# Attention's steps a turn later, copies behind a projection later, and level products in any free PSUM pair

## What is computed

```python
h = rms_norm_2(x, norm_pre[layer])
proj = h @ w_in[layer]
y_a = gla_branch(...)          # gated linear scan, 4 heads, both directions
for block of 128 queries:      # diff_branch, 4 heads
    s = einsum(q, k)           # two score maps, c = 0 and 1
    p = softmax(s)
    o = (p[0] - lam * p[1]) @ v
y_c = hgrn_branch(...)         # gated linear scan, 4 heads, both directions
y = concatenate([y_a, y_b, y_c]) @ w_out[layer]
x = x + rms_norm_2(y, norm_post[layer])
```

## Time and profile before

| | us |
|---|---|
| runs shown | 4494.43, 4501.37, 4509.14 (median 4501.37) |
| the profiled execution's own time | 4500.21 |
| its span (first to last instruction) | 4498.4 |
| PE / DVE / ACT / POOL busy in the span | 3923.6 / 1992.3 / 1439.2 / 958.7 |
| mean granted PE clock, share of full speed | 0.931 |

### The profile page before, as it was taken

The page is one execution under the profiler, slowest core; times in us unless marked ns, Lnnn a source line. Parts: engine busy times, 40 slices in busy tenths (PEclk is TensorE's granted clock), DMA queues, the critical chain, the costliest instruction groups (busy, mean ns, idle before and its releaser), DMA issues.

```text
span 4498.4 us, 66792 instructions
## 1 busy us (share of the span) xinstructions
PE 3923.6 (87%) x29404; PEld 2409.6 (54%) x29404; DVE 1992.3 (44%) x2165; ACT 1439.2 (32%) x1795; POOL 958.7 (21%) x426
## 2 busy tenths in 40 slices
PE   6988899999989999988997978988787978978777
PEld 3555565666656665455444555555444455555444
DVE  2456455555454642432224354263642264264542
ACT  4222323233232322222113323333444232343442
POOL 2313333232333322031132201111002210111002
PEclk8999999999999999999998988989888989989899
DMA  2111111111111112432212000100012100100002
GB/s 92 53 39 39 48 39 53 39 53 45 43 50 42 57 49 84 159 122 103 104 69 86 30 10 19 33 15 24 19 52 76 34 10 10 43 19 20 24 8 101
DMA packets 61585, 226.93 MB, mean 50 GB/s; under 512 B 6832, under 2 KB 8560, under 8 KB 60784
## 3 DMA queue, kind: packets, MB, share of 16 engines
q1 hardware_dynamic: 50064, 181.77, 11.7%
q10 hardware_dynamic: 11232, 40.90, 2.3%
HBM read 174.93 MB, written 47.71 MB: 49 GB/s over the span
## 4 chain that ended last, share of the span: by engine, by line
PE 71%; DVE 16%; ACT 9%; DMA 2%; issue 1%; POOL 1%; ACTq 0%; DVEq 0%; SPq 0%; POOLq 0%
PE psum L955 69%; DVE arena L2038 6%; ACT arena L1524 5%; DVE arena L2041 4%; DVE arena L2493 2%; DVE arena L2430 2%; PE psum L958 2%; ACT L1524 1%; ACT wh L1524 1%; DMA arena<-in_w_proj_conv 1%; DVE arena L2045 1%; ACT arena L1979 1%; DVE hl L2038 0%; ACT hh L1524 0%; POOL wl L2548 0%
## 5 line engine op out<-in xcount | busy, mean ns | idle before, releaser
L955 PE MATMUL psum<-arena 64*64 64x32 f32 (+11 forms) x19116 | 1589.3, 283 | 390.4 <-ACT arena L1524 186.2
L955 PEld LDWEIGHTS psum<-arena 64*64 64x64 f32 (+5 forms) x19116 | 1109.5, 158 | 878.5 <-issue 448.8
L2548 POOL TENSOR_TENSOR wl<-arena,wh 128x1024 bf16<-128x1024 f32 (+1 forms) x195 | 474.7, 2434 | 2405.4 <-ACT wh L1524 2403.6
L955 PE MATMUL psum<-hh,wh 128*128 128x512 f32 x3120 | 891.4, 432 | 98.6 <-ACT arena L1524 24.7
L1524 ACT ACTIVATE arena<-psum 128x512 f32<-128x512 f32 (+4 forms) x660 | 415.8, 630 | 1393.7 <-PE psum L955 1055.3
L955 PE MATMUL psum<-hh,wl 128*128 128x512 bf16 x3120 | 784.0, 394 | 1.2 <-POOL wl L2548 1.2
L955 PEld LDWEIGHTS psum<-hh,wh 128*128 128x128 f32 x3120 | 607.0, 200 | 301.7 <-issue 58.6
L2038 DVE TENSOR_TENSOR arena<-psum,arena 128x512 f32<-128x512 f32 (+3 forms) x488 | 319.3, 654 | 973.7 <-PE psum L955 628.1
L955 PE MATMUL psum<-hl,wh 128*128 128x512 bf16 x3120 | 736.0, 383 | 5.6 <-POOL hl L2548 5.5
L2041 DVE SCALAR_TENSOR_TENSOR arena<-arena 128x1024 f32<-128x1024 f32 x356 | 573.9, 1612 | 83.1 <-ACT arena L1524 69.9
L2548 POOL TENSOR_TENSOR arena<-arena 128x1024 f32<-128x1024 f32 (+4 forms) x142 | 362.6, 2553 | 955.1 <-ACT arena L1524 467.9
(11 more groups left out here) (38 smaller groups left out, 834.1 us busy)
## 6 DMA issues: line engine op xcount, KB each, us to landing
arena<-in_w_in SPq DMA_DIRECT2D x161, 512.0 KB, 3.5
scr_g<-arena ACTq DMA_DIRECT2D x24, 512.0 KB, 2.6
arena<-scr_g SPq DMA_DIRECT2D x24, 512.0 KB, 4.4
arena<-in_w_out SPq DMA_DIRECT2D x24, 512.0 KB, 3.5
arena<-in_w_mem_kv SPq DMA_DIRECT2D x16, 512.0 KB, 3.5
scr_x<-arena SPq DMA_DIRECT2D x16, 512.0 KB, 3.6
arena<-scr_x SPq DMA_DIRECT2D x16, 512.0 KB, 7.4
arena<-in_x SPq DMA_DIRECT2D x8, 512.0 KB, 10.3
```

The source lines that it names most:

```text
L955: return pe.e.matmul(o, l, r, start=start, stop=stop)
L2548: return pool.seq.tensor_tensor(o, a, b, op)
```

## The change

- `attend`: `dw` is split. `dr` (DVE: reciprocal and the tiny product) comes after `WT`; `e1` (ACT) does the scaling of EX[z] one long step later; `dw` (DVE) keeps the multiply-add alone and stands in the next turn, behind that turn's `qk`. `dmax` and `dexp` follow `qk` after one short step each (a short step advances the fillers once, a long one twice). The score pairs are kept until `dexp`.
- Between `dexp` and `dv` the levels and diagonals may take any of the four pairs (`room`, ANY).
- `copied`: the copy behind eight scan projections a layer and behind all `dvp` and `dqk` projections comes half a yield later, and the pair is kept until then. `dvp`, `dqk` and `dg` projections go in parts of 3 matmuls, each a quarter of a yield.
- `grow`: the two products on KG come first, then the two on QF, then the two of the tree; `xk` and `kt` wait for those on KG, `lev` for those on QF.
- `PACE` and `BESIDE` have other values. Loads are placed up to three ahead. The roots `fin` and `pre0` are made in the other order, `consts2` waits for `pre0`'s sum, and the sum `pre1` of the second layer takes a pair of UPPER instead of LOWER.

```diff
         self.owed += n
         while self.owed >= 1 and self.live:
-            self.owed -= 1
             try:
-                next(self.g)
+                self.owed -= next(self.g) or 1
             except StopIteration:
                 self.live = False
 
...
-        for f, *n in fillers:
-            f.step(n[min(stage or 0, len(n) - 1)])
+    for share in main:
+        for f, n in fillers:
+            f.step(n * (share or 1))
 
 
...
+    LOWER, UPPER, ANY = (0, 4), (4, 8), (0, 8)
...
-    def P(key, src, h, n=S, m=128, back=False, among=LOWER, deep=2):
+    def P(key, src, h, n=S, m=128, back=False, among=LOWER, deep=2, share=None):
 
 
         PROJ[key] = (src, h, n, m, back)
         steps = (n + 511) // 512 * 8 * (1 if h is None else 3)
         deep = deep if h is None else 3 * deep
         for part in range(steps // deep):
-            yield
+            yield share
...
-        for t in tags[::-1]:
+        for t in tags:
             do("stat_sum", t)
             do("stat_end", t)
         ps.leave(("stat", tag))
...
-    def held(step, use):
-
-        ps.take(use, 2, LOWER)
+    def held(step, use, among=LOWER):
+
+        ps.take(use, 2, among)
         ps.keep(use, 2)
         do(*step)
+
+    room = {"levels": LOWER}
+
+    def copied(g, key, *step):
+
+        yield from g
+        ps.keep(("proj", key), 2)
+        yield 0.5
+        do(*step)
+        ps.leave(("proj", key))
 
...
-                do("sv_copy", L, t, i)
+                key = ("sv", L, t, i)
+                yield from copied(P(key, w[ct], f"p{L}", deep=4), key, "sv_copy", L, t, i)
                 yield
...
-                held(("diag", L, t, g, p), ("diag", L, t, g, p))
+                held(("diag", L, t, g, p), ("diag", L, t, g, p), room["levels"])
...
                 for g, p in parts:
-                    held(("lev", L, t, lv, g, p), ("lev", L, t, lv, g, p))
+                    held(("lev", L, t, lv, g, p), ("lev", L, t, lv, g, p), room["levels"])
                     yield
                     if (g, p) == parts[-1]:
                         do("grow", L, t, lv)
...
 
-        yield from P(("dvp", L, h), A["w_in_2"][L][14 + h], f"p{L}", deep=4)
-        do("dv_copy", L, h)
-        yield
+        key = ("dvp", L, h)
+        yield from copied(P(key, A["w_in_2"][L][14 + h], f"p{L}", deep=1, share=0.25), key, "dv_copy", L, h)
+        yield 0.5
         two(("dv_turn", L, h), ("dv_turn", L, h))
...
     def qk_ready(L, h):
 
         for i in range(2):
-            yield from P(("dqk", L, h, i), A["w_in_2"][L][6 + 4 * i + h], f"p{L}", deep=4)
-            do("dq_copy", L, h, i)
-            yield
+            key = ("dqk", L, h, i)
+            yield from copied(P(key, A["w_in_2"][L][6 + 4 * i + h], f"p{L}", deep=1, share=0.25), key, "dq_copy", L, h, i)
+            yield 0.5
             held(("rope", L, h, i), ("rope", L, h, i))
-            yield
+            yield 0.5
             do("turned", L, h, i)
             ps.leave(("rope", L, h, i))
...
-        yield from between(P(("dg", L, h), A["w_in_2"][L][18 + h], f"p{L}", deep=4), None, ("do_norm", L, h))
+        yield from between(P(("dg", L, h), A["w_in_2"][L][18 + h], f"p{L}", deep=1, share=0.25), None, None, None, ("do_norm", L, h))
...
     def attend(L, n):
 
+
         (h, q), last = divmod(n, 8), divmod(n - 1, 8)
         if n < 32:
             for c in range(2):
                 ps.take(("ds", L, h, q, c), 2, UPPER)
+                ps.keep(("ds", L, h, q, c), 2)
             do("qk", L, h, q)
+        if n:
+            do("dw", L, *last)
+        yield True
+        if n < 32:
             for c in range(2):
                 do("dmax", L, h, q, c)
-            yield
+        yield True
+        if n < 32:
             for c in range(2):
                 do("dexp", L, h, q, c)
+                ps.leave(("ds", L, h, q, c))
+            room["levels"] = ANY
             yield
         if n:
             for g in range(2):
                 one(("dt", L, *last, g), ("dt", L, *last, g), UPPER)
-        if n < 32:
-            do("dw", L, h, q)
-        yield
-        if n:
+            yield
             for g in range(2):
                 do("WT", L, *last, g)
+        if n < 32:
+            do("dr", L, h, q)
         yield
+        if n < 32:
+            do("e1", L, h, q)
+            if n == 0:
+                yield
         if n:
             one(("dv", L, *last), ("dv", L, *last), UPPER)
+        room["levels"] = LOWER
+        if n:
             yield
             do("do", L, *last)
             yield
 
 
-    PACE = (0.6, 0.57, 0.54, 0.54)
-    BESIDE = ((1, 2, 3, 2, 3, 3, 3, 2), (5, 6, 4, 3, 0, 0, 1, 6), (3, 4, 3, 4, 3, 1, 0, 0), (0, 2, 3, 3, 3, 2, 2, 0))
+    PACE = (0.62, 0.59, 0.555, 0.555)
+    BESIDE = ((1, 2, 2.3, 2.4, 2.4, 2.4, 2.6, 2.8), (5, 5.5, 4.5, 3, 0, 0, 4, 4), (3.2, 3.2, 3.2, 3.2, 2.2, 1, 1, 1.6), (1, 2, 3, 3, 3, 2, 2, 0))
...
         ahead, pace = Filler(scan(L)), PACE
         first = Filler(norms_fin() if L == 0 else iter(()))
+        first.step(2)
         for g in (dv_ready(L, 0), qk_ready(L, 0)):
             weave(g, (ahead, 1.2), (first, 2.0))
         for n in range(33):
             h, q = divmod(min(n, 31), 8)
             if n < 32 and q == 0:
                 other = Filler(beside(L, h))
-            for _ in attend(L, n):
-                ahead.step(pace[h])
-                other.step(BESIDE[h][q] / 6)
-                ahead.step(pace[h])
+            for short in attend(L, n):
+                for _ in range(1 if short else 2):
+                    ahead.step(pace[h])
+                    other.step(BESIDE[h][q] / 12)
...
-            run(stat("pre1", S))
+            run(stat("pre1", S, UPPER))
...
-    fill(2)
+    fill(3)
...
-        fill(begun + 2)
+        fill(begun + 3)
...
-                    pe.wait_ge(*at("grow", L, t, lv - 1))
+                    pe.wait_ge(*at("grow_q", L, t, lv - 1, 1))
...
-            pe.wait_ge(*at("grow", L, t, 6))
+            pe.wait_ge(*at("grow_k", L, t, 6, 1))
...
-                act.wait_ge(*at("grow", L, t, lv - 1))
+                act.wait_ge(*at("grow_k", L, t, lv - 1, 1))
...
+        def e1(L, h, q):
+            z = q % 2
+            act.wait_ge(*at("dr", L, h, q))
+            f(EX[z], EX[z], AF.Copy, scale=DST[:, 16 * z + 6:16 * z + 7]).then_inc(*act.up("e1", L, h, q))
+
...
@@ -2436,12 +2464,15 @@
             dve.wait_ge(*at("xk", L, t, lv))
             dve.wait_ge(*at("lev", L, t, lv, 1, 1 if t == 0 else 0))
             m = 1 << lv
+            T, n = [tree(d, lv) for d in range(2)], 512 >> lv
             for d in range(2):
-                T = tree(d, lv)
-                tt(half(KG[d], d, m), half(KG[d], d, m), T[:, :, 1 - d:2 - d].to_broadcast([128, 512 >> lv, m]), MUL).then_inc(*dve.up("grow_k", L, t, lv, d))
-                tt(half(QF[d], 1 - d, m), half(QF[d], 1 - d, m), T[:, :, d:d + 1].to_broadcast([128, 512 >> lv, m]), MUL).then_inc(*dve.up("grow_q", L, t, lv, d))
-                x = tt(tree(d, lv + 1, True).unsqueeze(2), T[:, :, 0:1], T[:, :, 1:2], MUL)
-                x.then_inc(*dve.up(*(("grow", L, t, lv) if d else ("grow_0", L, t, lv))))
+                k = half(KG[d], d, m)
+                tt(k, k, T[d][:, :, 1 - d:2 - d].to_broadcast([128, n, m]), MUL).then_inc(*dve.up("grow_k", L, t, lv, d))
+            for d in range(2):
+                q = half(QF[d], 1 - d, m)
+                tt(q, q, T[d][:, :, d:d + 1].to_broadcast([128, n, m]), MUL).then_inc(*dve.up("grow_q", L, t, lv, d))
+            for d in range(2):
+                tt(tree(d, lv + 1, True).unsqueeze(2), T[d][:, :, 0:1], T[d][:, :, 1:2], MUL).then_inc(*dve.up("grow_t", L, t, lv, d))
...
-        def dw(L, h, q):
+        def dr(L, h, q):
             z = q % 2
             s = DST[:, 16 * z:16 * z + 16]
             dve.wait_ge(*at("dexp", L, h, q, 1))
             dve.seq.reciprocal(s[:, 6:8], s[:, 4:6]).then_inc(*dve.up("dw_rec", L, h, q))
-            tt(s[:, 8:9], s[:, 7:8], sc[:, 4:5], MUL).then_inc(*dve.up("dw_lam", L, h, q))
-            ts(EX[z], EX[z], s[:, 6:7], None, MUL).then_inc(*dve.up("dw0", L, h, q))
+            tt(s[:, 8:9], s[:, 7:8], sc[:, 4:5], MUL).then_inc(*dve.up("dr", L, h, q))
+
+        def dw(L, h, q):
+            z = q % 2
+            s = DST[:, 16 * z:16 * z + 16]
+            dve.wait_ge(*at("e1", L, h, q))
             stt(EX[z], EX[2], s[:, 8:9], EX[z], MUL, ADD).then_inc(*dve.up("dw", L, h, q))
...
@@ -2719,7 +2754,7 @@
             sp.e.dma_start(scr["x"][ct], BC[:, ct, :]).then_inc(*sp.land("x_out2" if ct < 2 else "x_out", 0, ct))
 
```

More of the change, by code:

```diff
@@ L161, in weave @@
 def weave(main, *fillers):
-    for stage in main:
-        for f, *n in fillers:
-            f.step(n[min(stage or 0, len(n) - 1)])
+    for share in main:
+        for f, n in fillers:
+            f.step(n * (share or 1))
 def build(nc, ctx, A, out):
@@ L319, in pair @@
         return bank(use, 1024)
-    LOWER, UPPER = (0, 4), (4, 8)
```

(20 more changed lines are left out.)

## The result

The changed kernel takes 4535.8 us (median) against 4497.9 us for the kernel before on the same chip: a ratio of 1.0079, 95% interval 1.0057 to 1.0102. It is 0.8% slower where 4402 us, 2% faster, was forecast. The profiled execution has a span of 4535.1 us.

What follows compares the result with a forecast made beforehand. PE, busy for 87% of the span, was taken to set the end, with idle time mostly in the two mixing stretches. 92 us there, 11 at the second layer's first projection, less 5 at the start: 4402 us, range 4330 to 4470.

Steps and rivals of the forecast that it cites:

- The rest: Outside the mixing stretches: loads three ahead, mostly barred by NSP = 3, cost 0, from -3 to +3 us.
- the 5 us for the start: Program start: the third load ahead of `init` delays x's DMAs and loses 5 us (3 to 7).
- the second layer's first projection: With `pre1`'s sum in UPPER, PE need not wait for `norm_pre`: 11 us won (6 to 12).
- the 92 us: Both mixing stretches: 34 us less idle time and 12 us from the clock a layer, 46 for each of two layers.
- The order of `grow`: Mixing stretches: `xk` and `kt` may start sooner, 22 + 4 us of idle time a layer.
- The later copies: Mixing stretches: copies half a step later and parts of 3 matmuls, 3 us of idle time a layer (-3 to +8).
- The turn of attention: Mixing stretches: `dw` a turn later, its scaling moved from DVE to ACT, 4 us of idle time a layer.
- the free pairs: Mixing stretches: levels may take any unread pair instead of waiting for L2430, 12 us of idle time a layer.
- The pairs stay taken: Rival, mixing stretches: levels find no free pair, so 12 us a layer and their clock are missing; 4426 us, chance 0.10.
- The waits move: Rival, mixing stretches: sooner levels wait for L2430 instead, a quarter of the idle time goes; 4466 us, chance 0.13.
- `e1` blocks ACT's queue: Rival, mixing stretches: the scaling, waiting for `dr`, holds ACT up to 4.3 us, 64 times; slower, chance 0.07.
- The clock did not stay up: Rival judged: both mixing stretches run at 0.97, saving 118 us of busy time instead of 24; 4308 us, chance 0.08.

Runs made afterwards that it cites:

- e1: The changed kernel with weight loads placed two ahead again instead of three: 4398.2 us, 0.9778 of before.
- e2: The kernel before with only the loads placed three ahead: 4696.0 us, 1.0441 of before.
- e6: e2 with a projection's weight slot counted as free one plan step later: 4603.7 us, 1.023 of before.
- f2: e1 with the old order of `grow` and its old waits: 4415.3 us, 0.9812 of before.
- e4: The kernel before with only the new order of `grow` and its three waits: 4494.8 us, 0.9989 of before.
- f3: e1 with copies directly behind their projections and the old parts of 12 matmuls: 4447.6 us, 0.9901 of before.
- f4: e1 with the old `attend` and `dw` and no ANY, so levels in the lower pairs: 4478.7 us, 0.9971 of before.
- f1: e1 with the levels kept to the lower pairs instead of ANY: 4424.7 us, 0.9833 of before.
- g2: e1 with the scaling on DVE instead of ACT: 4391.6 us, 0.9756 of before.
- h2: g1 with the scaling on DVE instead of ACT: 4377.0 us, 0.9731 of before.
- e5: The kernel before with weight DMAs three ahead, ACT's and POOL's conversions still two ahead: 4498.3 us, 0.9993 of before.
- g1: e1 with weight conversions one ahead, DMAs still two ahead: 4362.3 us, 0.9692 of before.
- h1: The kernel before with conversions one ahead, DMAs two ahead: 4494.5 us, 0.9993 of before.

## Why the prediction was wrong

**The step that failed** is in "The rest": "Elsewhere three loads ahead is already barred by NSP = 3 wherever two projections are open; in single file ACT's copy of the weights comes ahead of the result's copy: 0, from -3 to +3." The slots do bar a fourth load, but the moment at which one becomes free is the last part of a projection. With `begun + 2` the load then often waited for the next projection to begin; with `begun + 3` it goes into the plan at that very moment, and its weight copy is queued on ACT ahead of the result's copy. The text named the instruction, the place and the 1.06 us, and then costed it at nothing without naming what hid it. It measured 137 us in the changed plan (e1, the start's 5 to 7 us among them) and 198 in the old one (e2). The 1.06 us cost more than themselves since they come between the end of a projection and the copy that PE waits for, and since PE's clock falls in the longer waits: over the changed kernel's first 2467 us 22 of the 49 lost us are busy time. What part of the loss comes so and what part by other work behind the conversions stays open (e6).

**The sum of the rest came out by luck, its terms did not.** Without that edit the change gives 4398 us, where the forecast without the 5 us for the start is 4397. The mixing stretches gained 52 and 38 us for a predicted 46 each, most of it idle time of PE (about 40 and 38 us for 34), and the second layer's first projection 12.7 us (136.4 to 123.7) for 11: it starts, as predicted, about 1 us after high part 0, released by ACT's `hh` and no longer by `norm_pre`. The other order of the roots gained 1.6 us for 0 (0.5 to 1.6 in the versions with it). The start lost 6.5 us at x's last tile for a predicted 5.

Inside the 92 us three terms were mis-sized. The order of `grow`, more than half of the sum, is worth 17 us (f2), and nothing that can be measured alone (e4); the row with 3.88 us of wait was read as if nothing else were late there. The later copies, 6 us with clock, are worth 49 (f3). The turn of attention, 8 us, is worth 54 (f4 less f1). Both were taken from order in an in-order queue, of which the prediction saw the 235.8 us of ACT's waits and did not price it. Only the free pairs (26 for 24) came out. Terms too large and too small cancelled. Undoing the parts one at a time costs 17 + 49 + 80 = 146 us where all together gave 100, of which some 13 are outside the mixing stretches. So they are not a sum; it fits this that each matters more once the others have made room, as `grow` does (17 us here, nothing alone).

Two workings of the prediction don't hold by themselves. Its own price of 34 us idle to 46 with clock turns the bound of 60 us a layer into 4332 us, not 4345. And the earlier trace rows doesn't show the same 16 matmuls twice: one row has operands of 32 rows, the other of 64. The reading stands all the same, since the granted clock over the two rows is 1.00 and 0.50.

**The rivals.** "The pairs stay taken" is refuted by f1. "The waits move" holds for `grow` alone (e4). "`e1` blocks ACT's queue" named the right queue and the wrong instruction: with the scaling taken off ACT nothing changes (g2), or it gets worse (h2). The clock did not stay up; in the mixing stretches it is 0.90 and 0.91 in e1 and 0.89 in the changed kernel. The 20 us that the prediction worked out for DVE's shorter instruction, beside the rule of the Trainium skill (Perfetto Trace Analysis, Optimizing Scalar/DVE Operations), are not what the runs show: -7 us within the noise, and +15 us, the other way, in the fastest kernel.

## What to carry to other kernels

A prefetch has a place in the in-order queue of every engine that takes part in it, and each is worth placing by itself. Here the DMA could go early at no measurable cost (e5), while a conversion that waits for a slot to be released cost 137 and 198 us when it stood too early. One step later still gained 36 us in the changed plan (g1) and nothing in the old one (h1), so how late is right has to be tried. When an instruction that waits is moved ahead in a queue, cost it by what stands behind it, not by its duration. And when several edits are made at once, one that looks like mere tidying ("three ahead instead of two") can hide the gain of all the others.

## What the runs showed that was not expected

The same 24 matmuls took 3.13 and 5.85 us at the same place of the program, after waits of 1.11 and 2.25 us: one microsecond more of waiting was followed by nearly the whole group at 1.2 GHz (granted clock 0.51 over it). In both kernels an equal piece of work and a wait of 7 to 8 us stood ahead of this. And two programs whose queues on PE, DVE, ACT and POOL are in the same order, before and e5, had spans of 4498.4 and 4486.3 us in their profiled executions and 920.0 and 908.0 us in the first mixing stretch, while the medians of their executions are the same (0.9993). So a difference of ten microseconds between two single executions, in either direction, says nothing here, and the gains of single stretches above are no finer than that.
